# 96 instead of 128 slots for an expert's rows in a mixture-of-experts decoder layer

## The reference

```python
g_idx = argmax(xf @ w_group + b_group)                  # 1 of 4 groups
e_in_group = (xf @ w_expert + b_expert)[g_idx]           # 8 experts of that group
top_v, top_i = lax.top_k(e_in_group, 2)                  # 2 of the 8
gate = p_g * softmax(top_v)
eid = g_idx * 8 + top_i                                  # 2048 (token, expert) pairs on 32 experts
# per expert e, on the rows xb that chose it:
h = silu(xb @ w1[e]) * (xb @ w3[e])                      # 1024 -> 512
y = h @ w2[e]                                            # 512 -> 1024
out[token] += y * gate
```

## Time and profile before

| | before |
|---|---|
| median of 3 runs | 1163.4 us (1162.27 to 1164.91) |
| the profiled execution | 1164.24 us |
| its span in the profile | 1162.1 us |
| mean granted TensorE clock | 0.977 of full speed |
| PE busy | 1096.3 us (94%), 5766 matmuls |
| DVE, ACT, POOL busy | 900.1, 718.6, 139.7 us |

### The profile page before, as it was taken

One profiled execution on the slowest core, in us unless ns is written; L12 is line 12 of the kernel. 1 busy time (PEld: TensorE's weight loads), 2 busy tenths in 40 slices (PEclk: granted clock), 3 DMA queues, 4 the chain that ended last, 5 costly groups with the idle time before them and its releaser, 6 DMA issues. The chain is left out here.

```text
span 1162.1 us, 16798 instructions
## 1 busy us (share of the span) xinstructions
PE 1096.3 (94%) x5766; PEld 894.9 (77%) x5766; DVE 900.1 (77%) x1033; ACT 718.6 (62%) x882; POOL 139.7 (12%) x192
## 2 busy tenths in 40 slices
PE   8999999999999899997999999999999999999950
PEld 7887777778777668885878888888888888888840
DVE  5505957678575772567989999999999999999947
ACT  5423555646643571112878888888888888888830
POOL 1001000010000120001021110111111111101000
PEclk9999999999999999997999999999999999999985
DMA  7111231313213253003999999999999999999529
GB/s 232 46 35 39 90 89 59 107 39 107 67 46 95 103 214 142 37 37 133 425 427 422 396 384 396 386 384 396 382 383 390 382 392 383 390 387 387 214 77 375
DMA packets 77117, 275.29 MB, mean 237 GB/s; under 512 B 20752, under 2 KB 51600, under 8 KB 63888
## 3 DMA queue, kind: packets, MB, share of 16 engines
q1 hardware_dynamic: 66272, 253.69, 57.6%
q0 software_dynamic: 9216, 16.80, 3.8%
q10 hardware_dynamic: 1584, 4.20, 0.9%
HBM read 259.57 MB, written 31.85 MB: 251 GB/s over the span
## 5 line engine op out<-in xcount | busy, mean ns | idle before, releaser
L1198 DVE TENSOR_TENSOR e_lo<-W,e_hi 128x1024 fp32r<-128x1024 f32 x384 | 451.9, 1219 | 24.5 <-ACT e_hi L1192 21.7
L1192 ACT ACTIVATE e_hi<-W 128x1024 fp32r<-128x1024 f32 x384 | 403.4, 1060 | 94.7 <-PE ps L1163 88.7
L1161 PE MATMUL ps<-e_hi,xT_hi 128*128 128x512 f32 x496 | 196.3, 396 | 1.9 <-DVE xT_lo L1920 1.0
L1163 PE MATMUL ps<-e_lo,xT_hi 128*128 128x512 f32 x496 | 193.7, 390 | 0.0
L1162 PE MATMUL ps<-e_hi,xT_lo 128*128 128x512 f32 x496 | 193.1, 389 | 0.0
L472 PE MATMUL ps<-xnT_hi,w_hi 128*128 128x512 f32 x320 | 129.0, 403 | 1.6 <-DVE u L861 0.6
L472 PE MATMUL ps<-xnT_hi,w_lo 128*128 128x512 f32 x320 | 128.0, 400 | 0.0
L472 PE MATMUL ps<-xnT_lo,w_hi 128*128 128x512 f32 x320 | 125.3, 392 | 0.0
L900 DVE TENSOR_TENSOR_SCAN kept<-kept,start_at 128x1024 f32<-128x1024 f32 (+7 forms) x64 | 88.9, 1389 | 29.1 <-ACT kept L702 29.1
L1161 PEld LDWEIGHTS ps<-e_hi,xT_hi 128*128 128x128 f32 x496 | 93.5, 189 | 20.9 <-DVE xT_lo L1920 1.2
L1163 PEld LDWEIGHTS ps<-e_lo,xT_hi 128*128 128x128 f32 x496 | 93.1, 188 | 19.9
(11 more groups left out here) (244 smaller groups left out, 1706.9 us busy)
## 6 DMA issues: line engine op xcount, KB each, us to landing
W<-in_w_dram SPq DMA_DIRECT2D x96, 2048.0 KB, 15.2
w_raw<-in_w_in_dram SPq DMA_DIRECT2D x20, 512.0 KB, 4.1
yy<-y_rows SPq DMA_DIRECT2D x7, 1024.0 KB, 12.7
xt<-in_x_dram SPq DMA_DIRECT2D x8, 512.0 KB, 3.7
w_out_raw<-in_w_out_dram SPq DMA_DIRECT2D x8, 512.0 KB, 6.4
xn_rows<-xn SPq DMA_DIRECT2D x8, 512.0 KB, 2.6
out_dram<-x ACTq DMA_DIRECT2D x7, 512.0 KB, 9.1
x<-in_x_dram SPq DMA_DIRECT2D x2, 1536.0 KB, 10.7
```

The lines of the kernel that those rows point to most:

```text
L1161: pe.matmul(o, xs_hi[:, k], e_hi[:, p, cols], start=(k == 0), stop=False)
L1163: mm = pe.matmul(o, xs_hi[:, k], e_lo[:, p, cols], start=False, stop=(k == last))
L1192: act.activation(e_hi[:, p], flat[:, p * D:(p + 1) * D], ACT.Copy).then_inc(s["hi_made"], 1)
L1198: dve.tensor_tensor(e_lo[:, p], flat[:, p * D:(p + 1) * D], e_hi[:, p], ALU.subtract).then_inc(s["lo_made"], 1)
```

## The change

An expert's round has 96 slots instead of 128 (`ROWS`). The rows of an expert beyond 96 go to further parts, of which there can be `NBLK` = 11 (before 8), and up to `OVER` = 21 overflow rounds (before 15). `COLS` becomes 352 (before 256). As 96 is no power of two, a rank's part is found as (rank * 683) >> 16, and its slot as rank - 96 * part. Tiles that hold slots as partitions or columns shrink to 96, those that have a column per (part, expert) grow to 352 or 320, and some move in SBUF.

```diff
-    NBLK = S // P
-    OVER = PAIRS // P - 1
+    ROWS = 3 * P // 4
+    NBLK = -(-S // ROWS)
+    OVER = PAIRS // ROWS
+    PART_UP, PART_SHIFT = 683, 16
...
-        of_slot = [place(f"of_slot{i}", [P, P], F32R) for i in range(NOH)]
+        of_slot = [place(f"of_slot{i}", [P, ROWS], F32R) for i in range(NOH)]
...
-        xg = [place(f"xg{i}", [P, D]) for i in range(2)]
-        xT_hi = place("xT_hi", [P, KT, P], F32R)
+        xg = [place(f"xg{i}", [ROWS, D]) for i in range(2)]
+        xT_hi = place("xT_hi", [P, KT, ROWS], F32R)
...
+        eye = ident[0:ROWS, 0:ROWS]
+        turned_x = lambda k: ps[:, k // 4, k % 4 * ROWS:(k % 4 + 1) * ROWS]
+        whole_x = ps[:, 0:2, 0:4 * ROWS]
...
-                mm = pe.transpose(psf[:, k * P:(k + 1) * P], xg[b][:, k:D:KT], ident)
+                mm = pe.transpose(turned_x(k), xg[b][:, k:D:KT], eye)
...
-            pe_product(pe, s, start, *xT_of(n), [ps[:, 2]], 2, KT - 1)
+            pe_product(pe, s, start, *xT_of(n), [ps[0:ROWS, 2]], 2, KT - 1)
...
-                mm = pe.transpose(ps[:, 4, k * P:(k + 1) * P], hid[:, k:F:FT], ident)
+                mm = pe.transpose(ps[:, 4, k * ROWS:(k + 1) * ROWS], hid[:, k:F:FT], eye)
...
-            pe_product(pe, s, start, hidT_hi, hidT_lo, [ps[:, 5], ps[:, 6]], 1, FT - 1)
+            pe_product(pe, s, start, hidT_hi, hidT_lo, [ps[0:ROWS, 5], ps[0:ROWS, 6]], 1, FT - 1)
...
-            act.activation(xT_of(n)[0].rearrange("p k t -> p (k t)"), psf[:, 0:D], ACT.Copy).then_inc(s["xT_hi_made"], 1)
+            act.activation(by_bank(xT_of(n)[0]), whole_x, ACT.Copy).then_inc(s["xT_hi_made"], 1)
...
-                pool.iota(past, [[P, NBLK - 1], [0, NE]], base=P, channel_multiplier=0, **small_ints).then_inc(iotas, 1)
+                pool.iota(past, [[ROWS, NBLK - 1], [0, NE]], base=ROWS, channel_multiplier=0, **small_ints).then_inc(iotas, 1)
...
-                        pe.matmul(ps[:, TABLE, 0:COLS], of_slot[n % NOH], of_column[n % NOH],
+                        pe.matmul(ps[0:ROWS, TABLE, 0:COLS], of_slot[n % NOH], of_column[n % NOH],
...
-                    link(dve.tensor_copy(rank_i[:, :, ms], rank_f[:, :, ms]))
-                    link(dve.tensor_scalar(low_i[:, :, ms], rank_i[:, :, ms], P - 1, None, ALU.bitwise_and))
-                    link(dve.tensor_copy(slot[:, :, ms], low_i[:, :, ms]))
-                    link(dve.tensor_scalar(part_i[:, :, ms], rank_i[:, :, ms], 7, None, ALU.arith_shift_right))
+                    link(dve.tensor_scalar(rank_i[:, :, ms], rank_f[:, :, ms], float(PART_UP), None, ALU.mult))
+                    link(dve.tensor_scalar(part_i[:, :, ms], rank_i[:, :, ms], PART_SHIFT, None, ALU.arith_shift_right))
+                    link(dve.scalar_tensor_tensor(slot[:, :, ms], part_i[:, :, ms], -float(ROWS), rank_f[:, :, ms], ALU.mult, ALU.add))
```

More of the change, by code:

```diff
@@ L62, in hymba_moe_layer @@
     PAIRS = 2 * S
-    NBLK = S // P
-    OVER = PAIRS // P - 1
+    ROWS = 3 * P // 4
+    NBLK = -(-S // ROWS)
+    OVER = PAIRS // ROWS
+    PART_UP, PART_SHIFT = 683, 16
+    assert all(r * PART_UP >> PART_SHIFT == r // ROWS for r in range(S)) and S * PART_UP < 1 << 24
     LOG = NG + NE
@@ L1111, in hymba_moe_layer @@
         room[:] = [128 * KIB, 164 * KIB]
-        xg = [place(f"xg{i}", [P, D]) for i in range(2)]
-        xT_hi = place("xT_hi", [P, KT, P], F32R)
[L1114 to L1119, removed]
+        xg = [place(f"xg{i}", [ROWS, D]) for i in range(2)]
+        xT_hi = place("xT_hi", [P, KT, ROWS], F32R)
+        xT_lo = place("xT_lo", [P, KT, ROWS], F32R)
+        act_out = place("act_out", [ROWS, F])
+        hid = place("hid", [ROWS, F])
+        hidT_hi = place("hidT_hi", [P, FT, ROWS], F32R)
+        hidT_lo = place("hidT_lo", [P, FT, ROWS], F32R)
+        y = [place(f"y{i}", [ROWS, D]) for i in range(2)]
         x1_kib = (128 * KIB + 24 * KIB) / KIB
-        x1T_hi = at("x1T_hi", x1_kib, [P, KT, P], F32R)
-        x1T_lo = at("x1T_lo", x1_kib + 4, [P, KT, P], F32R)
+        x1T_hi = at("x1T_hi", x1_kib, [P, KT, ROWS], F32R)
+        x1T_lo = at("x1T_lo", x1_kib + 4, [P, KT, ROWS], F32R)
         xT_of = lambda n: (x1T_hi, x1T_lo) if isinstance(n, int) and n == 1 else (xT_hi, xT_lo)
+        eye = ident[0:ROWS, 0:ROWS]
+        turned_x = lambda k: ps[:, k // 4, k % 4 * ROWS:(k % 4 + 1) * ROWS]
+        whole_x = ps[:, 0:2, 0:4 * ROWS]
+        by_bank = lambda t: t.rearrange("p (b k) t -> p b (k t)", b=2)
         PIECES = KT * F // D
@@ L1128, in hymba_moe_layer @@
         e_lo = at("e_lo", 64, [P, PIECES, D], F32R)
-        idx_token = [keep(f"idx_token{i}", [P, 1], I32) for i in range(2)]
-        idx_pair = [keep(f"idx_pair{i}", [P, 1], I32) for i in range(2)]
+        idx_token = [keep(f"idx_token{i}", [ROWS, 1], I32) for i in range(2)]
+        idx_pair = [keep(f"idx_pair{i}", [ROWS, 1], I32) for i in range(2)]
         assert KT * F == FT * D
@@ L1213, in act_silu @@
             act.wait_ge(s["hidden"], n)
-            act.activation(act_out, ps[:, 2], ACT.Silu).then_inc(s["silu"], 1)
+            act.activation(act_out, ps[0:ROWS, 2], ACT.Silu).then_inc(s["silu"], 1)
         def act_y(act, s, n, b, rounds, down_start):
@@ L1546, in first_gate @@
                     pe.wait_ge(half_lo_made, 1)
-                    pe_product(pe, s_e, 0, xT_hi, xT_lo, [ps[:, 2]], 2, KT - 1, (0, 1))
+                    pe_product(pe, s_e, 0, xT_hi, xT_lo, [ps[0:ROWS, 2]], 2, KT - 1, (0, 1))
                     pe.wait_ge(s_e["xT_made"], 1)
-                    pe_product(pe, s_e, 0, xT_hi, xT_lo, [ps[:, 2]], 2, KT - 1, (2, 3))
+                    pe_product(pe, s_e, 0, xT_hi, xT_lo, [ps[0:ROWS, 2]], 2, KT - 1, (2, 3))
                 def round_of(e, b, rounds, last=False):
@@ L1919, in _ @@
                     half = lambda t: t[:, 4 * h:4 * h + 4].rearrange("p k t -> p (k t)")
-                    dve.tensor_tensor(half(xT_lo), ps[:, h], half(xT_hi), ALU.subtract).then_inc(lo_half, 1)
+                    dve.tensor_tensor(half(xT_lo), ps[:, h, 0:4 * ROWS], half(xT_hi), ALU.subtract).then_inc(lo_half, 1)
                 round_of(0, 0)
```

37 lines of the change are left out of this document (18 added, 19 removed).

## The result

The changed kernel took 1173.63 us (median of 6 runs, 1171.9 to 1176.94); the kernel before, beside it, 1163.53 us (6 runs, 1162.27 to 1165.78). The ratio is 1.0086, with a 95% interval of 1.0068 to 1.0104: it is slower by 10.0 us (8 to 12). Forecast were 1161.8 us and a range of 1154.0 to 1165.5 us. The profiled execution of after took 1174.64 us, with a span of 1172.5 us against 1162.1.

What follows compares the result with a forecast made beforehand. PE was taken as the bound in the expert stage. Transposes -1.7, router +0.5 and +0.2, router to first product -0.2, end -0.4 sum to -1.6 us, from 1163.4 to 1161.8 us; range 1154.0 to 1165.5 us.

Steps and rivals of the forecast that it cites:

- I take 0 for the distance of 0.2265 us: Experts' products on PE: fewer stationary columns leave the distance between starts unchanged; 0 us, at most 7.6 us saved.
- Gathers and scatters carry only valid rows, so their bytes stay: Experts' indirect DMAs: 96 slots instead of 128 leave the bytes moved unchanged, so no cost was counted.
- The transposes: Experts' rounds on PE: only the last transpose of a group gains, 0.027 us twice a round, -1.7 us in all.
- Router, in PE and DVE: Router before the experts: wider table products cost PE +0.5 us; ranks, one-hots and the last table product together +0.2 us.
- Six more empty iterations: Overflow loop at the end: further empty iterations lie in waits of SP and DVE and cost nothing.
- ACT and DVE: Splits in a round: 0.52 us less on DVE, about 0.2 us on ACT; PE waits for neither, so counted as nothing.
- the end: After the last round's transposes: PE's 1.63 us wait for splits falls by 0.26 us, the last scatter's issue by 0.1.
- (a): Rival, chance 0.17: the 13 ns above streaming time in each product distance go with the stationary width, giving 1154.2 us.
- (b): Rival, chance 0.09: all the experts' transposes shrink as their moving side does, giving 1153.1 us.
- (c): Rival, chance 0.07: PE pays 0.09 us at four borders between 96-row and 128-row instructions each round, giving 1173.3 us.
- (d): Rival, chance 0.02: some expert has more than 96 rows, so an overflow round follows, giving over 1181 us.
- (e): Rival, chance 0.07: DVE's longer chain around the first product or the ranks is 1 to 4 us worse, 1163 to 1166 us.

Runs made afterwards that it cites:

- gather96: The kernel before, with only gathers and scatters cut to the first 96 rows; 1167.5 against 1164.88 us, ratio 1.0016.
- both96: The kernel before, with 96-column expert products and 96-row transposes in the old memory layout; one execution, 1167.69 us.
- prod96: The kernel before, with only the experts' products narrowed to 96 of 128 stationary columns; 1169.28 against 1165.05 us, ratio 1.0043.
- turn96: The kernel before, with only the experts' transposes narrowed to 96 rows; 1165.26 against 1165.05 us, ratio 1.0012.
- router96_rows128: The changed kernel with experts' tiles, transposes, products, tables, lists, gathers and scatters back at 128; 96 slots, 352 columns, 21 loops stay; 1165.57 us, ratio 1.0008.
- prod64: The kernel before, with experts' products narrowed to 64 stationary columns, leaving out some slots that hold rows; one execution, 1167.85 us.
- stride128: The changed kernel with 512 instead of 384 bytes between parts of the stationary tile, products still 96 columns; 1173.57 against 1164.55 us, ratio 1.0068.

## Why the prediction was wrong

**The step that failed** is "I take 0 for the distance of 0.2265 us", with its bounds of 0 to -7.6 us and "Upward I find no reason". The mean distance went from 0.2275 to 0.2314 us (from 0.2265 to 0.2317 in the stretches shown). In a round this is +0.187 us for the width and +0.089 us for the packed tile; 30 to 31 such rounds make +8.3 to +8.6 us. The argument looked at the load's length, saw it hidden beside the product, and concluded that a shorter load could only help. The runs show a distance that does not follow the load's length: a load takes 134 ns with 64 columns, 161 with 96 and 188 with 128, always less than a distance, and yet 96 columns are dearer than 128 and 112 dearer than 96. Each width has a repeating pattern of its own, and 128 columns have the tightest of the six; why is open. A step that changes the shape of the bounding instruction needed an upper bound too. The nearest rows for it were those behind each group of transposes, where the same kernel takes 5 or 6 distances of 228 to 236 ns before it settles. The prediction read its 0.2265 us in a settled stretch and found that "there is nothing else in a round"; the rows with one decimal hid that its sum of 17.7 us is short of 17.753 by these distances and by the wide pair (0.315 to 0.319 us) behind each group.
The 0.2133 us for 512 columns, from which those bounds start, do agree with the runs: at half of full speed products of 512 columns start 427 ns apart (after from 12.1 us, gather96 from 591.2 us), 1.2 columns per ns, and half of 427 is 213.5 ns. The rest of the distance at full speed was taken to be fixed or to go with the columns; it was 14.0, 15.4, 16.5 and 19.6 ns on average for 128, 104, 96 and 120 columns and followed neither.

**The second is** "Gathers and scatters carry only valid rows, so their bytes stay". The bytes did stay (16.80 and 16.79 MB); the cost of nothing did not follow. In rounds that the DMA bounds, 96-row transfers lowered the rate by a sixth, +1.9 us in the total by gather96 (0.5 to 3.3), +2.4 us by the first rounds' losses. Why they do is open. The earlier trace rows show ACT waiting 4.1 us for weights and PE 1.0 us for the split piece behind them, so the first rounds were known to have no cover.

**Right:**
- The transposes: the pair after a group 0.03 us nearer, no gain from those inside, -0.053 us a round (both96 against prod96), where 2 x 0.027 was forecast. As forecast, it takes both the shorter load and the shorter transpose; with 128-column products the pair stayed and the round was 0.020 us longer (turn96).
- Router, in PE and DVE: from the first product of the output projection to the last table product 132.3 us before and 132.8 us after, where +0.5 and +0.2 were summed; router96_rows128, which has all of that and nothing of the rest, 1.0008, or +0.9 us (-0.3 to +2.2). The scan took 0.82 us for 0.62 in the earlier trace rows, at most 0.27 more as bounded, and the gather's issue 1.20 for 1.46. From the last table product to the first product of the experts 0.2 us were to be gained. It is 9.1 us before and 8.7 after, but 8.8 to 10.5 us in the kernels with the old router, so the profiles cannot tell.
- Six more empty iterations: nothing.
- ACT and DVE: shorter by what was worked out (1213 to 944 ns, 691 to 557 ns), and hidden, since PE stays the bound.

Not right, but too small to matter: the end. PE's wait for the last splits was forecast to fall by 0.26 us and stayed, 1.66 against 1.63 us.

**The rivals.** (a) fell with prod64. (b) fell with the transposes' distance. (c) has nearly the time that was measured, 1173.3 us, but not its reason: turn96 holds its four borders and costs 0.020 us a round, prod96 has the same borders of width and its first pair is no longer than before (316 and 315 to 319 ns). Its price need not have been one of shape either: the 0.32 us of the earlier trace rows stand behind every group of transposes of before as well (0.315 to 0.319 us), where 128 rows and columns follow 128. The agreement in time is chance. (d) did not occur, and (e) neither. The measured mechanism was none of the rivals; (c)'s chance of 0.07, an estimate of the author's, was the only one on that side with such a price.

**The account of the 10.0 us:** width +5.6 to +5.8 and packed layout +2.7 to +2.8, less 1.6 for the transposes, in all some 6.9 (31 x 0.223); 96-row DMAs 1.9; the router 0.9. Sum 9.7 us. In after's own profile, less the 2.8 us of low clock ahead of the change, 7.6 us are found, since its first rounds lost but 0.2 us more than before's. The sum stands within the interval of 8 to 12 us, but 1.9 and 0.9 have wide intervals of their own (0.5 to 3.3, -0.3 to 2.2), so only the 6.9 us of the rounds are well known.

No version tried was faster than the kernel before. What is left of the change in router96_rows128, with 128 columns in the products and 128-row DMAs, costs at most 0.2% and gains nothing.

## What to carry to other kernels

Where the tensor engine is the bound, as here with products of 512 columns 227.5 ns apart at full clock, narrowing the stationary operand saved nothing here and cost 0.5 to 2.2% of a round: keep 128 columns and the unpacked layout, or measure the distance for each width, as it does not go evenly with it. Price an edit that changes the shape of the bounding instruction upward as well as downward. And a gather of fewer rows need not be a cheaper gather (gather96: 1.0016 of before's time, and 351 GB/s instead of 429 from 560 to 570 us): look at the GB/s of the stretch in which the weights come late, not at the bytes and not at the DMA share alone. Before a few us between two profiles are given to the edit, compare the stages that the edit does not touch and their granted clock.

## What the runs showed of the hardware that was not expected

- A product of 512 columns in a dense row starts every 226.7 ns with 128 stationary columns once it has settled (227.5 on average), and every 228.9 to 233.1 ns on average with 64 to 120, at the full granted clock and with the load hidden. From cheap to dear the order is 128, 104, 96, 64, 112, 120.
- The layout counts: the packed tiles, with 384 and not 512 bytes between parts, cost +0.089 us in a round of 72 products, +1.2 ns each (after against stride128). Which part of the layout does it is not separated.
- Indirect DMAs of 96 rows slow the packets of another queue: 16-KB packets from about 615 to about 670 ns on average, by a third of them that take over 650 ns, and 429 to 351 GB/s (gather96). Why they do is not shown; no run tells which DMA engine wrote where.
